# The recurrent mixer of a two-block network on one core: scan inputs one tile ahead of their gate products, scans three tiles back, the last gate product split around tile 7's gates

## What is computed

```python
def recurrent_mixer(x, w_in, conv_w, conv_b, gate_a_w, gate_a_b, gate_x_w, gate_x_b, a_param, w_out):
    gate, xr = jnp.split(x @ w_in, [1024], axis=-1)
    xr = causal_depthwise_conv(xr, conv_w, conv_b)              # 4 taps
    h = rg_lru(xr, gate_a_w, gate_a_b, gate_x_w, gate_x_b, a_param)
    return (h * jax.nn.gelu(gate)) @ w_out

def rg_lru(x, ...):                                             # 8 blocks of 128 channels
    r = sigmoid(block_diag(x, gate_a_w, gate_a_b))
    i = sigmoid(block_diag(x, gate_x_w, gate_x_b))
    log_a = -8.0 * r * softplus(-a_param)
    a = exp(log_a); u = sqrt(-expm1(2.0 * log_a)) * (i * x)
    h = associative_scan(linear_combine, (a, u), axis=1)        # h[t] = a[t] * h[t-1] + u[t]
```

## Time and profile before

| | |
|---|---|
| median of 3 runs | 2814.07 us (2813.23 to 2816.17) |
| the profiled execution, its own time | 2815.08 us |
| its span | 2813.3 us |
| PE busy | 2785.0 us, 99% of the span |
| DVE, ACT, POOL busy | 44% each |
| the recurrence in the span | about us 668 to 804 |

### The profile page before, as it was taken

One profiled execution on the slowest core, in us unless ns is written; L12 is line 12 of the kernel. 1 busy time (PEld: TensorE's weight loads), 2 busy tenths in 40 slices (PEclk: granted clock), 3 DMA queues, 4 the chain that ended last, 5 costly groups with the idle time before them and its releaser, 6 DMA issues.

```text
span 2813.3 us, 32448 instructions
## 1 busy us (share of the span) xinstructions
PE 2785.0 (99%) x12950; PEld 2265.7 (81%) x12950; DVE 1246.7 (44%) x2089; ACT 1237.8 (44%) x1805; POOL 1232.0 (44%) x549
## 2 busy tenths in 40 slices
PE   9999999999999999999999999999999999999998
PEld 8886888888778888887777888888877778888887
DVE  4666552544765525336666432021256674420112
ACT  4665442444754334334674443143345744342331
POOL 4222444444554444443455444444434564444443
PEclk9999999999999999999999999999999999999999
DMA  4212332333223323332222323333322222333332
GB/s 152 91 64 65 92 103 90 105 98 97 90 82 98 105 90 99 100 97 80 76 68 90 98 91 97 97 97 98 105 88 71 68 90 90 98 98 98 98 97 75
DMA packets 74726, 259.25 MB, mean 92 GB/s; under 512 B 9856, under 2 KB 9856, under 8 KB 74576
## 3 DMA queue, kind: packets, MB, share of 16 engines
q1 hardware_dynamic: 73280, 255.08, 28.8%
q10 hardware_dynamic: 1296, 2.10, 0.2%
HBM read 254.95 MB, written 2.13 MB: 91 GB/s over the span
## 4 chain that ended last, share of the span: by engine, by line
PE 93%; DVE 3%; ACT 2%; POOL 1%; issue 1%; DMA 0%; SPq 0%; DVEq 0%; ACTq 0%; POOLq 0%
PE ps L442 27%; PE ps L443 27%; PE ps L444 27%; PE ps L508 2%; PE ps L538 2%; PE ps L564 1%; PE ps L521 1%; PE ps L566 1%; PE ps L565 1%; PE ps L490 1%; PE ps L491 1%; PE ps L492 1%; PE ps L453 1%; DVE tmp L1845 0%; POOL w_lo L2007 0%
## 5 line engine op out<-in xcount | busy, mean ns | idle before, releaser
L2007 POOL TENSOR_TENSOR w_lo<-raw,w_hi 128x1024 fp32r<-128x1024 f32 x469 | 1132.5, 2416 | 1478.6 <-ACT w_hi L924 1478.5
L442 PE MATMUL ps<-xs,w_hi 128*128 128x512 f32 x2176 | 862.6, 396 | 1.6 <-DVE xs L1408 1.6
L443 PE MATMUL ps<-xs,w_hi 128*128 128x512 f32 x2176 | 847.9, 390 | 0.0
L444 PE MATMUL ps<-xs,w_lo 128*128 128x512 f32 x2176 | 847.8, 390 | 0.0
L924 ACT ACTIVATE w_hi<-raw 128x1024 fp32r<-128x1024 f32 x470 | 495.0, 1054 | 660.3 <-PE ps L444 620.9
L442 PE MATMUL ps<-hid,w_hi 128*128 128x512 f32 x1316 | 515.8, 392 | 5.6 <-POOL w_lo L2007 2.9
L443 PE MATMUL ps<-hid,w_hi 128*128 128x512 f32 x1316 | 512.8, 390 | 0.0
L444 PE MATMUL ps<-hid,w_lo 128*128 128x512 f32 x1316 | 512.8, 390 | 0.0
L442 PEld LDWEIGHTS ps<-xs,w_hi 128*128 128x128 f32 x2176 | 408.9, 188 | 97.2 <-issue 8.1
L443 PEld LDWEIGHTS ps<-xs,w_hi 128*128 128x128 f32 x2176 | 408.9, 188 | 88.9 <-issue 5.3
L444 PEld LDWEIGHTS ps<-xs,w_lo 128*128 128x128 f32 x2176 | 408.8, 188 | 85.7
(11 more groups left out here) (232 smaller groups left out, 2580.4 us busy)
## 6 DMA issues: line engine op xcount, KB each, us to landing
raw<-in_weights SPq DMA_DIRECT2D x470, 512.0 KB, 3.4
btab<-in_rel SPq DMA_DIRECT2D x8, 256.0 KB, 3.9
out<-tmp ACTq DMA_DIRECT2D x8, 256.0 KB, 2.0
hT<-in_x SPq DMA_DIRECT2D x3, 512.0 KB, 7.3
btab<-in_heads SPq DMA_DIRECT2D x6, 256.0 KB, 3.8
tmp<-in_heads SPq DMA_DIRECT2D x6, 256.0 KB, 3.8
common<-in_fixed SPq DMA_DIRECT2D x1, 642.0 KB, 10.7
hT<-in_x SPq DMA_DIRECT2D x2, 256.0 KB, 4.1
```

The costliest lines, as they stand in the source:

```text
L442: pe.matmul(banks[bank][:], wh, rh, start=(k == 0), stop=False)
L443: pe.matmul(banks[bank][:], wh, rl, start=False, stop=False)
L444: last = pe.matmul(banks[bank][:], wl, rh, start=False, stop=(k == len(specs) - 1))
L2007: gp.tensor_tensor(w_lo[:, n % NPAIR, :], raw[:, n % NRAW, :], w_hi[:, n % NPAIR, :].bitcast(F32), ALU.subtract).then_inc(*w_low.tick(n))
```

## The change

PE does x(0) first, then for c = 0 to 6 x(c+1), g(c), a(c), i(c); then pieces 0 and 1 of g(7), a(7), i(7), pieces 2 to 7 of g(7), and the output products, in the order 0, 1, 3, 4, 5, 2 up to piece 5. DVE takes per step `rec_3(c-3)`, x(c+1) with its low part, then the scale of g(c), then L1737 of c. ACT takes per step the conversions for x(c+1), the Exp and Sqrt pairs (now at c = 2, 4 and 6), the conversions for g(c), `rec_in(c+1)`, `rec_high(c+1)`, Gelu of c, and the three tanh of c. No instruction of the computation is added or dropped. Line numbers of the changed kernel are 3 to 12 higher (L924 is L932, L1446 is L1454, L1737 is L1746, L2007 is L2017).

```diff
@@ PE
-            def rec_0(c):
-                bg, bx = 2 * (c % 2), 2 * (c % 2) + 1
-                linear(bg, ("rec_g", c), mat("rec_w_in", 0, P * c), xr, x_chunk(2))
-                free[bg] = (act, ("rec_g", c))
-                if c == 0:
-                    root(2)
-                linear(bx, ("rec_x", c), mat("rec_w_in", 0, 1024 + P * c), xr, x_chunk(2))
-                free[bx] = (taps, ("rec", c))
+            def rec_x(c):
+                bank = 2 * (c % 2) + 1
+                linear(bank, ("rec_x", c), mat("rec_w_in", 0, 1024 + P * c), xr, x_chunk(2))
+                free[bank] = (taps, ("rec", c))
+
+            def rec_g(c, k0=0, k1=8):
+                bank = 2 * (c % 2)
+                linear(bank, ("rec_g", c), mat("rec_w_in", 0, P * c), xr, x_chunk(2), k0, k1)
+                free[bank] = (act, ("rec_g", c))
...
-            for c in range(8):
-                rec_0(c)
-                if c:
-                    rec_1(c - 1)
-            for o in range(2):
-                rec_out(o, 0, 3)
+            rec_x(0)
+            root(2)
+            for c in range(7):
+                rec_x(c + 1)
+                rec_g(c)
+                rec_1(c)
+            rec_g(7, 0, 2)
             rec_1(7)
-            for o in range(2, 6):
+            rec_g(7, 2, 8)
+            for o in rec_order:
                 rec_out(o, 0, 3)
@@ ACT
-            roots_of = {3: (0, 1), 5: (2, 3), 7: (4, 5)}
+            roots_of = {2: (0, 1), 4: (2, 3), 6: (4, 5)}
...
+            weights(("rec_x", 0))
+            root(2)
+            rec_in(0)
+            weights(("rec_x", 1))
+            rec_high(0)
+            for c in range(7):
+                weights(("rec_x", c + 1))
+                rec_2(roots_of.get(c, ()))
+                if c >= 4:
+                    rec_4(c - 4)
                 weights(("rec_g", c))
-                if c == 0:
-                    root(2)
-                rec_2(roots_of.get(c, ()))
-                if c >= 5:
-                    rec_4(c - 5)
-                weights(("rec_x", c))
-                if c < 7:
-                    rec_gate(c)
-                if c:
-                    weights(("rec_a", c - 1))
-                    weights(("rec_i", c - 1))
-                rec_in(c)
-                if c == 7:
-                    rec_gate(7)
-                if c:
-                    rec_1(c - 1)
-                if 0 < c < 7:
-                    rec_t(c - 1)
-                rec_high(c)
...
+                rec_in(c + 1)
+                weights(("rec_a", c))
+                weights(("rec_i", c))
+                rec_high(c + 1)
+                rec_gate(c)
+                rec_1(c)
+                rec_t(c)
@@ DVE
-            for c in range(8):
-                if c == 0:
-                    root(2)
-                if c >= 4:
-                    rec_3(c - 4)
-                scale(2 * (c % 2), ("rec_g", c), 2, ("rec_g", c))
-                rec_0(c)
-                if 0 < c < 7:
-                    rec_1(c - 1)
+            root(2)
+            rec_x(0)
+            for c in range(7):
+                if c >= 3:
+                    rec_3(c - 3)
+                rec_x(c + 1)
+                rec_g(c)
+                rec_1(c)
             rec_last(4)
+            rec_last(5)
             rec_1(7)
-            for c in range(5, 8):
-                rec_last(c)
+            rec_g(7)
+            rec_last(6)
+            rec_last(7)
```

More of the change, by code:

```diff
@@ L409, in program @@
         rows = scratch.rearrange("h (p c) -> (h p) c", c=16)
+        rec_order = (0, 1, 3, 4, 5, 2)
         def tensor(T):
@@ L711, in rec_out @@
                        lambda k: T.wait_ge(pool, ("rec_y", k)), k0, k1)
-            for c in range(8):
-                rec_0(c)
-                if c:
-                    rec_1(c - 1)
-            for o in range(2):
-                rec_out(o, 0, 3)
+            rec_x(0)
[5 more added lines that the diff above has]
+            rec_g(7, 0, 2)
             rec_1(7)
-            for o in range(2, 6):
+            rec_g(7, 2, 8)
+            for o in rec_order:
                 rec_out(o, 0, 3)
             for k in range(3, 6):
-                for o in range(6):
+                for o in rec_order:
                     rec_out(o, k, k + 1)
@@ L1214, in scalar @@
[L1214 to L1218, removed]
+            weights(("rec_x", 0))
[8 more added lines that the diff above has]
+                    rec_4(c - 4)
+                weights(("rec_g", c))
+                rec_in(c + 1)
[5 more added lines that the diff above has]
+                rec_t(c)
@@ L1219, in scalar @@
+            weights(("rec_g", 7))
             weights(("rec_a", 7))
             weights(("rec_i", 7))
+            rec_decay(4)
             rec_1(7)
             rec_t(7)
+            weights(("rec_g", 7), 2)
+            rec_4(3)
             rec_2((6, 7))
+            for o in rec_order[:2]:
+                weights(("rec_out", o))
+            rec_gate(7)
+            rec_4(4)
+            for o in rec_order[2:]:
+                weights(("rec_out", o))
             rec_decay(6)
-            rec_4(4)
@@ L1226, in scalar @@
-            for o in range(2, 6):
-                weights(("rec_out", o))
             rec_4(5)
             rec_decay(7)
-            for o in range(6):
+            for o in rec_order:
                 weights(("rec_out", o), 3)
             rec_4(6)
-            for o in range(6):
+            for o in rec_order:
                 weights(("rec_out", o), 4)
             rec_4(7)
-            for o in range(6):
+            for o in rec_order:
                 weights(("rec_out", o), 5)
@@ L1726, in rec_0, with rec_g @@
                     V.wait_ge(product, ("rec_i", c - 2))
-                if c == 7:
-                    rec_1(6)
                 take_low(hi_lo(hid, 8 + c % 2), xc, ("rec_x", c))
+            def rec_g(c):
+                scale(2 * (c % 2), ("rec_g", c), 2, ("rec_g", c))
             def ring(c):
@@ L2036, in gpsimd @@
             low_done["n"] += 1
-            through(("rec_g", 0))
-            for c in range(8):
-                weights(("rec_g", c))
-                if c >= 5:
-                    rec_4(c - 5)
-                if c >= 4:
-                    rec_3(c - 4)
-                weights(("rec_x", c))
-                if c:
-                    weights(("rec_a", c - 1))
-                    weights(("rec_i", c - 1))
+            through(("rec_x", 0))
+            weights(("rec_x", 0))
+            for c in range(7):
+                weights(("rec_x", c + 1))
+                if c >= 4:
+                    rec_4(c - 4)
+                weights(("rec_g", c))
+                if c >= 3:
+                    rec_3(c - 3)
+                weights(("rec_a", c))
+                weights(("rec_i", c))
+            weights(("rec_g", 7))
+            weights(("rec_a", 7))
+            weights(("rec_i", 7))
+            weights(("rec_g", 7), 2)
             rec_4(3)
             rec_3(4)
-            for o in range(2):
+            for o in rec_order[:2]:
                 weights(("rec_out", o))
-            weights(("rec_a", 7))
-            weights(("rec_i", 7))
             rec_4(4)
             rec_3(5)
-            for o in range(2, 6):
+            for o in rec_order[2:]:
                 weights(("rec_out", o))
```

3 lines of the change are left out of this document (1 added, 2 removed).

## The result

The changed kernel took 2827.92 us (median of 4 runs, 2827.28 to 2829.47), the kernel before, on the same chip, 2814.39 us (4 runs). The ratio is 1.0048 (95% interval 1.0036 to 1.0061): slower by 13.5 us, where 12.6 was forecast.

The account below looks back on a forecast made before the run. PE was taken to bound the kernel, busy 2785.0 of 2813.3 us, with at most 8.1 us to gain. Wait 19.0 plus clock 1.7 minus 8.1 gave + 12.6 on the median 2814.07: 2826.7 us, range 2816 to 2832.

Parts of the forecast that it names:

- Tile 1's tap behind slab 111's conversion: On ACT, x(2)'s first tap stands behind a conversion that waits for slab 108, so it starts at 697.2 us.
- The loop of 7.6 us: DVE and ACT: from first tap of x(c+1) through high part, low part, scale and Gelu to third tanh, 7.6 us.
- even steps 7.2 and 7.75 on top: At c = 2, 4, 6 ACT's conversions, Exp/Sqrt pair and output high part add 7.2 or 7.75 us before the next tap.
- `rec_3(0)` by turns: Tile 3: DVE and POOL take turns over two low parts, so `rec_3(0)` takes 8.2 us instead of 6.0.
- First wait of PE: Slab 116's conversion stands behind tile 3's third tanh: PE waits 5.3 us from 734.3; slab 117 about 1.6 us more.
- Tile 5: Odd step: 6.0 us for `rec_3`, then 0.7 and the loop's 7.6, ending at 765.8 us.
- a(7): PE stands some 9 us for x(7)'s low part, ready at 778.0; i(7) starts at 781.2 instead of 762.2, 19.0 us lost.
- Clock: One half-clock stretch of PE behind i(7), charged 1.7 us; the bounds took none and two.
- The tail at nothing: From i(7) to the output products, last inputs come half a microsecond early, so no cost; turns on POOL could cost 1 to 2.
- the loop keeps up: Rival: taps and tanh overlap more, PE loses at most a microsecond in the recurrence; 2807 us, chance 0.12.
- The loop lags but few turns: Rival: the DVE/ACT loop lags but POOL seldom blocks DVE; + 3.3 to + 5.5 us, 2818 us, chance 0.10.
- The tail breaks as well: Rival: inputs 6 and 7 late by over 2 us, or turns at every tile; + 18 or more, 2833 us, chance 0.08.

Follow-up runs that it names:

- e1: Changed kernel with ACT's conversions of the slabs that g(c) opens moved behind the first tap of x(c+1); 2821.08 us, ratio 1.0022 to the kernel before.
- e2: Changed kernel with Gelu and tanh of c ahead of the high part of x(c+1), DVE's scale of g(c) ahead of the taps; 2814.40 us, ratio 0.9998.
- e4: Changed kernel with g(7) whole again, ahead of a(7) on PE; 2828.30 us, ratio 1.0046 to the kernel before.
- e5: Changed kernel with rec_3 of tiles 0 to 3 writing the scan's second input into PSUM instead of SBUF; 2822.89 us, ratio 1.0025.
- e7: e6 with the end of the recurrence laid out anew on ACT, POOL and DVE, output tile 2 fourth; 2806.52 us, ratio 0.9967 to the kernel before.
- e6: Changed kernel with e2 and e5 together, x(7) first in the last step, Exp/Sqrt of tiles 4 and 5 behind tile 6; 2815.81 us, ratio 1.0003.
- e3: Changed kernel with DVE's multiplication L1746 for c = 2 to 5 moved behind the next step's rec_3; 2817.11 us, ratio 1.0008 to the kernel before.

## Why the prediction was right

Step by step; forecast times have the 1.63 us taken off.

1. **Tile 1's tap behind slab 111's conversion:** forecast 695.6, measured 695.61. In e1 it is free and comes 3.8 us sooner.
2. **The loop of 7.6 us, even steps 7.2 and 7.75 on top:** measured 7.5, 7.22 (703.10 to 710.32) and 7.72 (733.91 to 741.63). The page "ScalarE: Activation LUTs" of the Trainium skill (What ACT_TABLE_LOAD costs) would have made the even steps 2.76 us longer with its drain; the runs don't agree with it. The sum left out a third table load of the even steps, that of the Gelu behind the Sqrt (714.11 to 715.39 at c = 2). It costs nothing only because it just fits while ACT waits for the scale of g(c), which ends at 715.43; that was luck.
3. **`rec_3(0)` by turns, 8.2 us:** measured 7.9. The order of the turns was right too (L1758 waits for the first low part, the next operation for the second).
4. **First wait of PE, 5.3 us at slab 116:** 4.8. The 1.6 us more at slab 117 did not show as a wait: PE lost 1.7 us there at half clock and met the slab in time. Half clock and a wait for data didn't add up here: slab 117's low part ended at 744.52, and PE got to it at 744.65.
5. **Tile 5 was undersized.** The sum took 6.0 us for `rec_3` there, as in the earlier trace rows; it took 8.8, since product, decay step and scan all met POOL. The first tap of x(7) was forecast at 772.0 and came at 774.05. That is the term that was off: 2.8 us, of which the earlier steps, a little shorter than forecast, gave back 0.7. It stood in the high bound, at 1.1 to 2.2 us.
6. **a(7): the size right, the releaser wrong.** I named x(7)'s low part, forecast at 776.4. It came at 778.62, and PE still did not start: a(7) needs bank 4 as well, which the tanh of a(6) freed at 780.44. Both hang on the same tile of the loop, and i(7) comes later than either (forecast 779.6, measured 782.00), so the sum did not feel it. The waits are laid out otherwise than forecast, too: 11.8 us at a(7) and not some 9, two small ones at a(6) and i(6) that I did not have, and none at i(7), where I named one as a sign: L1746 of tile 6 ended at 781.72, while PE still did a(7) at half clock. In e2, with the gates in the gap, the low part is the releaser. In the changed kernel a faster low part would have gained about 0.1 us by the rows: the scale behind it ended at 779.24, the table load that the Gelu needs as well at 779.13.
7. **Clock:** 1.7 us charged. The stretch behind a(7) cost 2.5, the one behind slab 116 another 1.7, in whose place PE would otherwise have waited for slab 117 (step 4).
8. **The tail at nothing:** no wait, and the cover was as thin as stated. Input 7's low part ended at 813.06; from i(7) PE has 29.9 us of work, to 811.9, and 1.8 us lost behind i(7), nearly all to the slower clock, brought it to 813.70. In e4, without that cover, the wait of 1.34 us appeared.

Sum: losses of 20.7 us forecast (19.0 + 1.7), 23.4 measured, against 8.1 and 8.5 before; + 12.6 against + 14.9 in the traces, the difference being mostly step 5. The spans differ by 13.3 us, since the trace of before came 1.6 us later to its root mark. That the medians, + 13.5, lie close to the forecast is thus partly luck: in the stretch that was summed the miss is 2.3 us.

The rivals: "the loop keeps up" fell because of the order in the lists and not of load, which e2 shows by moving three calls on ACT and one on DVE, with the same work on every engine. "The loop lags but few turns" fell at tiles 3 and 5; e5, with most of the turns gone, is 5.0 us faster, and the prediction had put 4.6 between its forecast and one turn lost a tile. "The tail breaks as well" fell by 0.6 us.

What the prediction did not ask is which orders on ACT, DVE and POOL would have let the change reach its own ceiling of 8.1 us. e7 reached it, with the change's order on PE but for one output tile moved.

## What to carry to other kernels

When a producer is moved one tile ahead, write down for each engine of the chain what stands between two of its visits, and compare the length of the whole turn, waits for each other included, with the bound engine's work per tile; busy shares of 44% say nothing about it. Fill the gaps in which one engine waits for another's part of the chain with the work of other tiles, and look at where an instruction that waits for the bound engine (here a weight conversion) stands ahead of one that feeds it. And when the loop is cured, look at once at the end of the stage: e6 was cured and had gained nothing over the kernel before, because everything the bound engine next needs was still timed for its old, later arrival.

## What the runs showed of the hardware that I had not expected

- A TENSOR_TENSOR_SCAN with both inputs in SBUF took 3.23 us beside a POOL operation of 2.57 us, against 1.22 us alone or with one input in PSUM. A TENSOR_SCALAR with one SBUF input, 0.42 us alone, took 2.62, 1.51 and, in e5, 2.04 us at the same places. In e5 the instruction ahead of it took its usual 0.69 us, so it was held itself and did not queue behind another's turn.
- The half clock began inside the long idle stretch and outlasted it: around the wait of 11.8 us the granted clock was at the lower level for 13.65 us, from 772.0 to 785.7, and PE ran at 0.43 us a matmul until then, 5.1 us after it had resumed. Behind the wait of 4.8 us it ran so for 3.4 us.
- e3 gained 7.4 us more than the edit's own arithmetic, since a shift of 2.5 us took `rec_3` out of POOL's way (7.9 us became 3.5 in tile 3): with contention of this kind the time of this kernel depended on small shifts more than on small costs.
